# Mixing stage: the last level's copies, the sigmoids' sums and the keys' squares go from VectorE to ScalarE, and three loads for attention stand later in SyncE's queue

## What is computed

```python
wlog = -softplus(-(w0 + tanh(xw) @ w2)) - 0.5
decay = exp(-exp(wlog))
a = sigmoid(a0 + xa @ a2)
g = sigmoid(xg) @ g2
kk = heads(k * k_k)
kk = kk * rsqrt(max(sum(kk * kk, axis=-1), 1e-24))
k = k * (1.0 + (a - 1.0) * k_a)
# per frame, state s of 64x64 per head, 8 heads, with a_t = -kk, b_t = kk * a:
sa = einsum('bhvk,bhk->bhv', s, a_t)
s = s * w_t + sa * b_t + v_t * k_t
y = einsum('bhvk,bhk->bhv', s, r_t)
```

## Time and profile before

| | us |
|---|---|
| median of 3 runs | 1564.22 |
| the runs | 1556.27 to 1564.59 |
| the profiled execution: its own time | 1559.99 |
| the profiled execution: span | 1558.2 |
| mean granted TensorE clock in it | 0.973 of full |
| PE busy, DVE busy, ACT busy | 93%, 58%, 29% of the span |

### The profile page before, as it was taken

How to read it: one execution, slowest core, us unless ns; L and a number is a source line. 1 busy time by engine, 2 the same in 40 slices (tenths; PEclk the granted TensorE clock), 3 DMA queues, 4 the chain that set the end, 5 groups by cost and what they waited for, 6 DMA issues and landing times. The chain is left out here.

```text
span 1558.2 us, 38960 instructions
## 1 busy us (share of the span) xinstructions
PE 1442.1 (93%) x16352; PEld 1002.5 (64%) x16352; DVE 905.1 (58%) x2027; ACT 452.5 (29%) x907; POOL 102.7 (7%) x103
## 2 busy tenths in 40 slices
PE   6999999999999999999987899979998799999994
PEld 4888888874565565556554566644554677777772
DVE  3555555566788899888975567645777123222220
ACT  2222222224333333333311344434554111111110
POOL 0000000000000000000000000000000222333321
PEclk9999999999999999999998899989999799999998
DMA  9522222536232132222121444437954999999961
GB/s 333 197 94 94 94 94 74 176 120 206 86 98 93 66 114 84 72 66 71 49 67 73 117 99 107 108 115 266 357 178 177 320 330 347 341 352 363 341 237 39
DMA packets 101936, 257.61 MB, mean 165 GB/s; under 512 B 35360, under 2 KB 54448, under 8 KB 92432
## 3 DMA queue, kind: packets, MB, share of 16 engines
q1 hardware_dynamic: 94032, 237.95, 44.5%
q0 software_dynamic: 7744, 17.33, 4.7%
HBM read 203.36 MB, written 60.56 MB: 169 GB/s over the span
## 5 line engine op out<-in xcount | busy, mean ns | idle before, releaser
L559 PEld LDWEIGHTS a_ps<-a_hT,a_wz 128*128 128x128 f32 x1792 | 202.6, 192 | 6.2 <-issue 3.8
L559 PE MATMUL a_ps<-a_hT,a_wz 128*128 128x128 f32 x1792 | 204.1, 275 | 1.7 <-DMA a_wz<-w_z 1.7
L2047 PE MATMUL d_ps<-late,last_down 128*128 128x512 f32 x256 | 116.8, 603 | 1.7 <-DVE last_down L1795 1.0
L2428 DVE TENSOR_SCALAR f_y<-f_down,table 96x512 f32<-96x512 f32 x32 | 23.9, 747 | 119.2 <-PE f_down L2222 65.1
L2229 DVE COPY f_xT<-f_turned 128x384 f32<-128x384 f32 x32 | 17.8, 558 | 125.9 <-PE f_turned L2196 125.9
L2047 PEld LDWEIGHTS d_ps<-late,last_down 128*128 128x128 f32 x256 | 47.2, 192 | 52.2 <-issue 50.8
L1553 ACT ACTIVATE late<-c_score,c_top 128x1024 f32<-128x1024 f32 (+8 forms) x72 | 50.6, 703 | 92.3 <-DVE c_top L1502 91.8
L1190 PE MATMUL b_ps<-b_wg,r_hT 128*128 128x512 f32 x128 | 66.8, 645 | 4.0 <-DMA r_hT<-hT_d 4.0
L890 DVE TENSOR_TENSOR b_M<-b_ps,r_causal 128x512 f32<-128x512 f32 x72 | 46.2, 682 | 33.1 <-PE b_ps L1253 33.1
L999 DVE STREAM_TRANSPOSE b_U<-b_T 64x256 f32<-64x256 f32 x144 | 63.3, 440 | 2.7
L1190 PE MATMUL b_ps<-r_wg,b_hT 128*128 128x512 f32 x128 | 64.1, 623 | 0.0
(11 more groups left out here) (380 smaller groups left out, 2812.2 us busy)
## 6 DMA issues: line engine op xcount, KB each, us to landing
wgu<-w_gate_up SPq DMA_DIRECT2D x15, 2048.0 KB
late<-w_gate_up SPq DMA_DIRECT2D x9, 2048.0 KB
wd<-w_down SPq DMA_DIRECT2D x17, 1024.0 KB
late<-w_down SPq DMA_DIRECT2D x10, 1024.0 KB
r_hT<-hT_d SPq DMA_DIRECT2D x16, 512.0 KB, 3.9
b_hT<-hT_d SPq DMA_DIRECT2D x16, 512.0 KB, 4.0
gate_d<-b_logits SPq DMA_DIRECT2D x32, 256.0 KB, 4.2
late<-gate_d SPq DMA_DIRECT2D x8, 1024.0 KB, 5.9
```

The costliest lines, as they stand in the source:

```text
L559: mm = pe.matmul(banks[Z_BANKS[n % 2]][:, j * P:(j + 1) * P], wz[:, i, (g + j) * P:(g + j + 1) * P], hT[t % 2][:, i, :], start=(i == 0), s ...
L2047: mm = pe.matmul(banks[2 + u][:], oT[t % 2][:, HB * branch(u) + k, :], wo[:, HB * branch(u) + k, half(u)], start=(k == 0), stop=(k == HB - 1))
```

## The change

- The last level's `low` copy (L972) and `merge` copy (L985) go from DVE to ACT, as `last_low` in slot 10 behind `copy_lower`, and `last_merge` in slot 11. `root` goes from slot 10, ahead of `copy_lower`, to slot 11, behind `last_merge`.
- DVE no longer adds the offsets (L846, L847). ACT's sigmoid reads the bank and takes the offset as a bias of one value per partition, so each 128x512 sigmoid becomes four of 128x128. PE's `gate` and `rows` wait for these sigmoids instead of the sums.
- The keys are squared by ACT (`squares`, slot 0, behind `copy_x`) and no longer by DVE (L842).
- PE's `low(s, 0)` gets an extra wait for the last `merged` of the turn before.
- SP's `load_head` moves behind the second item of turn `LAST`.

```diff
@@ sync
-                if s == LAST:
-                    sp.wait_ge(bon_done, NT)
-                    sp.wait_ge(v_turned, NT)
-                    load_head(sp, io, early, 0, 0, early["head_in0"])
-                for _ in range(6):
+                for item in range(6):
+                    if s == LAST and item == 2:
+                        sp.wait_ge(bon_done, NT)
+                        sp.wait_ge(v_turned, NT)
+                        load_head(sp, io, early, 0, 0, early["head_in0"])
@@ vector, keys_squared and sums
-                step(dve.tensor_tensor(kk[:], k_of(n), col(k_k, PAIRS), ALU.mult))
-                dve.tensor_tensor(kn[:], kk[:], kk[:], ALU.mult).then_inc(kk_sq, 1)
+                dve.tensor_tensor(kk[:], k_of(n), col(k_k, PAIRS), ALU.mult).then_inc(kk_ready, 1)
+                dve.wait_ge(kk_ready, n + 1)
-                dve.tensor_tensor(sig[:], paired(C0), col(w0, PAIRS), ALU.add).then_inc(w_sum, 1)
-                dve.tensor_tensor(av[:], paired(C1), col(a0, PAIRS), ALU.add).then_inc(a_sum, 1)
@@ vector, low and merge: the branches for i == NL - 1 become a return
-                    dve.tensor_copy(lo[:, 0:H // 2, :], solve[:, 0, 0:2 * P].rearrange("p (h i) -> p h i", h=H // 2)).then_inc(low_copied, 1)
-                    after(dve, w_done, t)
-                    dve.tensor_copy(U_right[0:HALF_T, :, :].rearrange("p (b h) i -> p b h i", b=2),
-                                    solve[0:HALF_T, :, 2 * P:].rearrange("p b (h i) -> p b h i", h=H // 2)).then_inc(merged, 1)
@@ scalar
+            def squares(n):
+                act.wait_ge(kk_ready, n + 1)
+                after(act, feats_ready, n)
+                act.activation(kn[:], kk[:], ACT.Square).then_inc(kk_sq, 1)
             def sigmoids(n):
-                act.wait_ge(w_sum, n + 1)
-                act.activation(sig[:], sig[:], ACT.Sigmoid).then_inc(w_sig, 1)
-                act.wait_ge(a_sum, n + 1)
-                act.activation(av[:], av[:], ACT.Sigmoid).then_inc(a_sig, 1)
+                act.wait_ge(lora_done, n + 1)
+                after(act, cs_ready, n)
+                after(act, e_ready, 3 * n)
+                after(act, inverse_ready, n)
+                for to, bank, off, done in ((sig, C0, w0, w_sig), (av, C1, a0, a_sig)):
+                    for p in range(PAIRS):
+                        ins = act.activation(to[:, p, :], banks[bank][:, p * P:(p + 1) * P], ACT.Sigmoid, bias=off[:, p:p + 1])
+                    ins.then_inc(done, 1)
+            def last_low(t):
+                act.wait_ge(low_done, NL * t + NL)
+                act.activation(low_of(NL - 1)[:, 0:H // 2, :], solve[:, 0, 0:2 * P].rearrange("p (h i) -> p h i", h=H // 2), ACT.Copy).then_inc(low_copied, 1)
+            def last_merge(t):
+                act.wait_ge(merge_done, NL * t + NL)
+                after(act, w_done, t)
+                act.activation(U_right[0:HALF_T, :, :].rearrange("p (b h) i -> p b h i", b=2),
+                               solve[0:HALF_T, :, 2 * P:].rearrange("p b (h i) -> p b h i", h=H // 2), ACT.Copy).then_inc(merged, 1)
@@ scalar, slot 0 behind copy_x; slots 10 and 11
+                        if there(n):
+                            squares(n)
-                        if k == 10:
-                            root(t)
                     if there(s) and k == 10:
                         copy_lower(s)
+                    if there(s) and levels_of(s) == NL:
+                        if k == 10:
+                            last_low(s)
+                        if k == 11:
+                            last_merge(s)
+                    if there(t) and k == 11:
+                        root(t)
@@ tensor
-                pe.wait_ge(w_sum, n + 1)
+                pe.wait_ge(w_sig, n + 1)
-                pe.wait_ge(a_sum, n + 1)
+                pe.wait_ge(a_sig, n + 1)
                     pe.wait_ge(T_ready, t + 1)
+                    after(pe, merged, NL * t)
```

More of the change, by code:

```diff
@@ L692, in mixing @@
         st = sb("st", [P, 2, H])
-        (set_done, lora_in, kk_sq, lora_done, gate_done, gate_copied, w_sum, w_sig, a_sum, a_sig, nn_ready, nn_root,
+        (set_done, lora_in, kk_sq, lora_done, gate_done, gate_copied, kk_ready, w_sig, a_sig, nn_ready, nn_root,
          cs_ready, e_ready, inverse_ready, feats_ready, v_turned, v_copied, rows_done, rows_copied, bon_done, bon_copied, wc_ready,
@@ L697, in mixing @@
          logits_done, logits_copied, bonus_ready, lower_copied, U_begun, no_logits, tail_in, dve_step) = (sem(n) for n in (
-             "set_done lora_in kk_sq lora_done gate_done gate_copied w_sum w_sig a_sum a_sig nn_ready nn_root "
+             "set_done lora_in kk_sq lora_done gate_done gate_copied kk_ready w_sig a_sig nn_ready nn_root "
              "cs_ready e_ready inverse_ready feats_ready v_turned v_copied rows_done rows_copied bon_done bon_copied wc_ready "
@@ L967, in low @@
             def low(t, i):
+                if i == NL - 1:
+                    return
                 dve.wait_ge(low_done, NL * t + i + 1)
                 lo = low_of(i)
-                if i == NL - 1:
-                    dve.tensor_copy(lo[:, 0:H // 2, :], solve[:, 0, 0:2 * P].rearrange("p (h i) -> p h i", h=H // 2)).then_inc(low_copied, 1)
-                    return
                 mask = spread(merge_mask[:, i, :].unsqueeze(1).unsqueeze(1), [P, 2, H // 2, Q])
```

## The result

| | before | after |
|---|---|---|
| median, us | 1562.82 (4 runs) | 1550.80 (4 runs) |
| lowest to highest | 1556.27 to 1564.59 | 1549.36 to 1552.16 |
| profiled execution: own time / span | 1559.99 / 1558.2 | 1549.36 / 1547.5 |
| mean granted clock in it | 0.973 | 0.973 |

After runs in 0.9933 of the time of before (95%: 0.9912 to 0.9954). The forecast was 1552 us, from 1543 to 1560.

What follows compares the result with a forecast made beforehand. PE was taken as the bound, with only its idle time to win and DVE's work limiting the gain at turn boundaries. -6.7 - 6.3 + 3.2 = -9.8 us, counted from 1562.1, gave 1552 us, range 1543 to 1560.

Steps and rivals of the forecast that it cites:

- Part 1: Turn boundaries: moving two solve copies off DVE gains 0.95 us at each of seven, -6.7 us in all.
- DVE's row: At turn boundaries: 12.5 us of DVE work without a wait, from PE's release to the end of the transposes.
- Part 2: Slots 0 to 2: offsets, sigmoids and squares moved from DVE to ACT gain 0 and cost 0.
- Part 3: Turn LAST: later attention loads remove PE's 3.97 us hT wait and the half clock behind it, -6.3 us.
- the row of 8.7 us: Turn LAST: the hT load landing after 8.7 us, against a median of 3.9, said to stand alone.
- Part 4: Behind turn boundaries: the clock falls to half at four instead of two, 1.6 us each, +3.2 us.
- (c): Turn LAST: the load move brings nothing; net -3.5 us, 1558.5 us; chance 0.09.
- (d): Turn boundaries: DVE's relief from further up reaches them, PE never waits there; about 1536 us; chance 0.06.
- (e): Turn boundaries: ACT's queue becomes the bound, making the kernel slower, 1574 us; chance 0.05.
- (a): Turn boundaries: the clock falls no more often than before; -13.0 us, 1549 us; chance 0.18.
- (b): Turn boundaries: the clock falls behind six or seven; +8.0 instead of +3.2, 1557 us; chance 0.14.

Runs made afterwards that it cites:

- e2: The kernel before with only the two copies out of solve on ACT and the root behind them: 1555.67 us beside 1559.84, ratio 0.9976.
- e6: The changed kernel with centred and variance moved from slots 9 and 10 to slot 7: 1545.59 us beside 1559.00 for before, ratio 0.9924.
- e7: The changed kernel with one part of the logits fill moved from slot 7 to slot 0: 1538.83 us beside 1559.00 for before, ratio 0.9870.
- e9: The changed kernel with one part of the logits fill moved from slot 0 to slot 7: 1566.51 us beside 1559.86 for before, ratio 1.0047.
- e3: The kernel before with only the offsets, sigmoids and squares moved to ACT: 1560.24 us beside 1559.84, ratio 1.0002.
- e1: The kernel before with only attention's three loads moved behind the second logits item of turn LAST: 1551.98 us beside 1559.84, ratio 0.9956.
- e4: The changed kernel with attention's three loads back at the start of turn LAST: 1555.10 us beside 1559.84 for before, ratio 0.9980.
- e5: The changed kernel with ACT's root back in slot 10 ahead of the copies: 1605.68 us beside 1559.00 for before, ratio 1.0300.

## Why the prediction was right

**Part 1, the copies.** The mechanism held and the size nearly: 0.92 us a turn against 0.95, e2 alone. The wait at `low` is 1.48 and not 1.39. ACT's copy took 0.38 us (0.43 assumed) and ended at 630.88, 1.0 us before PE needed it at 631.87, which is the cover that the sum gave. The reading that carried this is that the wait removed (1.41 us) was not the gain: the second chain, DVE's row, let only its own shortening through. e6, e7 and e9 bear the row out from three sides. What the sum did not see is the third chain, from the last product; it lies 0.75 us under the second, so it did not touch this change, but it held e6 back.

**Part 2, the sigmoids, offsets and squares.** Nothing was predicted and nothing came, e3 alone. Four biased sigmoids of 128x128 took 1.14 us (1.2 estimated), and the square ended at 643.31, 2.4 us ahead of L1232 at 645.71 (2.3 estimated).

**Part 3, the loads.** -6.8 us in the trace and -6.9 in e1, against -6.3. Both terms are there: no wait for hT, and the full clock in place of the half. The four parts of `outputs` behind the fills took 2.89 us and not 3.72, so 0.83 went where the sum had 0.5. In turn `LAST` nothing was next in line. One argument for this part was weaker than it looked: the row of 8.7 us does not stand alone. In before, three other loads of this tile, issued between 298 and 369 us, took 6.9 to 8.0 us to land; only from 400 us on is it by itself. e1 decides it.

**Part 4, the clock.** Three stretches at half clock with one double, where the sum had four single ones: +3.0 us against +3.2. That one trace came so close is luck. The time over that of seven undisturbed turns, from turn 1 to turn 8, was 4.1, 0.8 and 4.1 us in before, e1 and e3, and 7.1, 4.0 and 7.1 in after, e2 and e4: the mean rises by 3.0, but one trace may lie 3 us off. The direction and the order of size are shown by the granted clocks of all executions: 3.4 us more is missing with the wait of 1.48. e7 and e9 point the same way, since at 0.62 us the excess all but disappears and at 2.34 us every boundary pays; but they also move a part of the fill to or from the place just ahead of the wait, so they do not tell the idle time from what stands before it. The Trainium skill (TensorE: Matmul & The Clock Gate, "What's actually happening") gives the low clock as the default and as the state after an idle window. Here it also followed boundaries at which PE was never idle for longer than 0.93 us at once (before; 0.73 in e6), with matmuls in between, so by these traces it comes not only after idling.

**Not in the sum**: -1.35 us before turn 1, where PE waited 0.9 us for the weights a_wz instead of 1.7, and +0.9 us from attention on. The change touches neither place. From attention's first score to the end the eleven traces range from 697.8 to 703.0 us, so I take both for the spread between executions, without a run that shows it.

**The rivals.** (c), that the loads bring nothing, fell with e1; (d), that relief from higher up reaches the boundary, with e2 and e3. (e), ACT as the bound, is not what after does, but e5 shows that it is real: with the root ahead it costs 55 us, more than the 22 us beyond the forecast that I had given it, since the wait for `variance` comes first and not last. Between the forecast and (a) and (b) only the clock decides, and there the spread between single traces is as large as the difference; the clocks of all executions speak against (a), in which the loss would not have grown.

## What to carry to other kernels

When a wait goes, ask which chain comes second and by how much: here 2.34 us of idle time paid 0.92, because DVE had another row of work behind it that ended that much sooner and no more. Work that no one waits for, such as the logits' fills, was worth more directly in front of the wait that is left; moving one part of it brought 10 to 12 us, about as much as the whole change. And an instruction that waits in an in-order queue belongs behind those that others wait for: four lines of order on ACT make 55 us.

## What the runs showed of the hardware that I had not expected

- The granted clock fell more often the more idle time stood at a boundary, though no single idle time was above 2.4 us. With 0.62 to 0.73 us ahead of `low`, 1 of 13 boundaries was followed by half clock; with 2.34 us, 6 of 6. Against the same turn without one, a single stretch cost 1.6 to 1.7 us and a double one 3.0 to 3.1 (after, e4). So idle time came with a loss larger than itself: from e7 to after PE's waits ahead of `low` grow by 6.8 us and the time by 9.8 us by the ratios (12.0 by the medians), and from after to e9 by 6.9 us and 17.8 (15.7).
- The issue of a DMA on SP right behind the three large loads takes 3.72 us in before and 2.96 in e4; the same load ahead of them takes 0.43 in after. It lands 8.7 and 8.6 us after its issue began, against 3.9. So SP itself is held up, and with it the store and the load that stand behind. Why, no run here shows.
